# Weight sums of seven-product matrices made by accumulating transfers, with the signs moved to the other operand

## The reference, cut to what matters

```python
def sqrelu_mlp(h, w_up, w_down):
    a = jax.nn.relu(h @ w_up)
    return (a * a) @ w_down

def reference(x, ...):
    for i in range(DEPTH):                       # DEPTH = 2
        h = rmsnorm(x, norm_mix[i])
        x = x + (short_conv_mixer(...) if i % 2 == 0 else neighborhood_attention_2d(...))
        h = rmsnorm(x, norm_mlp[i])
        x = x + sqrelu_mlp(h, mlp_w_up[i], mlp_w_down[i])
    return rmsnorm(x, norm_final)
```

## Time and profile before

| | us |
|---|---|
| median of three runs | 1042.34 |
| the three runs | 1042.2, 1042.34, 1044.16 |
| span of the profiled execution, first to last instruction | 1041.8 |
| PE busy in it | 1032.3 |
| DVE busy | 846.8 |
| ACT busy | 598.4 |
| POOL busy | 103.6 |

### The profile page before, as it was taken

How to read it: one execution, slowest core, us unless ns; L and a number is a source line. 1 busy time by engine, 2 the same in 40 slices (tenths; PEclk the granted TensorE clock), 3 DMA queues, 4 the chain that set the end, 5 groups by cost and what they waited for, 6 DMA issues and landing times.

```text
span 1041.8 us, 15414 instructions
## 1 busy us (share of the span) xinstructions
PE 1032.3 (99%) x6104; PEld 905.4 (87%) x6104; DVE 846.8 (81%) x1185; ACT 598.4 (57%) x836; POOL 103.6 (10%) x158
## 2 busy tenths in 40 slices
PE   9999999999999999999999999999999999999997
PEld 8888888988998998998878888889888988988985
DVE  5876688699899689688987767797799798698697
ACT  6222347665584574575765655547664674674675
POOL 3453001000000000000113000000000000000003
PEclk9999999999999999999999999999999999999999
DMA  7998568326745645633998733157056547447423
GB/s 247 375 375 300 141 165 254 108 42 207 204 132 176 177 128 177 181 97 102 372 249 249 215 90 114 55 191 274 1 122 205 163 133 202 150 134 202 147 51 111
DMA packets 36998, 182.71 MB, mean 175 GB/s; under 512 B 5760, under 2 KB 5888, under 8 KB 22848
## 3 DMA queue, kind: packets, MB, share of 16 engines
q1 hardware_dynamic: 23184, 108.57, 28.8%
q0 software_dynamic: 13456, 72.64, 28.3%
q10 hardware_dynamic: 288, 0.52, 0.2%
HBM read 136.93 MB, written 27.32 MB: 158 GB/s over the span
## 4 chain that ended last, share of the span: by engine, by line
PE 93%; DVE 4%; DMA 1%; ACT 1%; issue 1%; POOL 0%; DVEq 0%; POOLq 0%; ACTq 0%
PE bank L770 29%; PE bank L771 29%; PE bank L772 29%; DMA raw<-sevens 1%; PE bank L975 1%; PE bank L953 1%; DVE w_l L1514 1%; PE bank L938 1%; PE bank L793 1%; DVE xs L1661 1%; PE bank L997 0%; DVE big L1970 0%; ACT big L1156 0%; DVE a_l L1727 0%; ACT w_h L1128 0%
## 5 line engine op out<-in xcount | busy, mean ns | idle before, releaser
L1128 ACT ACTIVATE w_h<-big 128x1024 fp32r<-128x1024 f32 x210 | 221.7, 1058 | 216.0 <-PE bank L772 215.0
L770 PE MATMUL bank<-a_h,w_h 128*128 128x256 f32 (+1 forms) x892 | 295.0, 331 | 0.0
L772 PE MATMUL bank<-a_h,w_l 128*128 128x256 f32 (+1 forms) x892 | 292.9, 328 | 0.0
L771 PE MATMUL bank<-a_l,w_h 128*128 128x256 f32 (+1 forms) x892 | 292.8, 328 | 0.0
L1514 DVE TENSOR_TENSOR w_l<-big,w_h 128x1024 fp32r<-128x1024 f32 x210 | 252.0, 1225 | 21.8 <-ACT w_h L1128 21.8
L770 PE MATMUL bank<-w_h,hx 128*128 128x512 f32 x568 | 222.1, 391 | 0.8 <-ACT big L1376 0.4
L771 PE MATMUL bank<-w_l,hx 128*128 128x512 f32 x568 | 221.2, 389 | 0.0
L772 PE MATMUL bank<-w_h,hx 128*128 128x512 f32 x568 | 221.0, 389 | 0.0
L770 PEld LDWEIGHTS bank<-a_h,w_h 128*128 128x128 f32 x892 | 169.6, 190 | 15.8 <-issue 0.2
L772 PEld LDWEIGHTS bank<-a_h,w_l 128*128 128x128 f32 x892 | 169.6, 190 | 15.0
L771 PEld LDWEIGHTS bank<-a_l,w_h 128*128 128x128 f32 x892 | 169.6, 190 | 14.7 <-issue 0.2
(11 more groups left out here) (193 smaller groups left out, 1253.6 us busy)
## 6 DMA issues: line engine op xcount, KB each, us to landing
big<-blocks SPq DMA_DIRECT2D x56, 1024.0 KB, 5.0
big<-big POOLq DMA_DIRECT2D x30, 1024.0 KB, 7.0
raw<-weights SPq DMA_DIRECT2D x52, 512.0 KB, 6.6
raw<-t_sums SPq DMA_DIRECT2D x16, 512.0 KB, 3.7
t_sums<-sevens POOLq DMA_DIRECT2D x6, 1024.0 KB, 12.6
t_sums<-t_sums POOLq DMA_DIRECT2D x6, 1024.0 KB, 12.2
raw<-sevens SPq DMA_DIRECT2D x12, 512.0 KB, 7.8
bias_tiles<-big POOLq DMA_DIRECT2D x8, 632.0 KB, 9.3
```

The lines of the kernel that those rows point to most:

```text
L770: nc.tensor.matmul(dst, sh, mh, start=start, stop=False, skip_group_check=again)
L771: nc.tensor.matmul(dst, sh, ml, start=False, stop=False, skip_group_check=again)
L772: return nc.tensor.matmul(dst, sl, mh, start=False, stop=stop, skip_group_check=again)
L1128: nc.scalar.activation(wh_all[:, w % SLOTS, :], src, ACT.Copy).then_inc(w_hi, 1)
```

## The change

The signs of the scheme are moved so that every sum of weights is a plain addition, and the subtractions fall on the operand sums and on the additions into the output (`ALU.subtract` in `evict` and `add`, `scale=-1.0` in one ReLU). The weight sums are now T1 = Y12 + Y11, T2 = T1 + Y22, T3 = Y12 + Y22 and T4 = Y21 + T2.

- T1 is made by POOL as an accumulating transfer of Y11 into Y12 (`first_sum`), for q+1 behind `add_sums(q)` in POOL's order.
- T2 stays with DVE (`sum_of_y`) in the same place; it now waits for the landing of T1's transfer.
- T3: once P1 has consumed Y11, POOL loads Y12 a second time from DRAM into the room of Y11, waits for it, and accumulates Y22 onto it.
- T4 is as before, but behind the longer T3 in POOL's order.

```diff
-                                  "P3": ("Y22", *loaded(q, "Y22")), "P5": ("Y12", t_sum, 2 * q + 1),
-                                  "P6": ("T2", t_sum, 2 * q + 2), "P7": ("Y11", t3_in, 16 * (q + 1)),
+                                  "P3": ("Y22", *loaded(q, "Y22")), "P5": ("Y12", t1_in, 16 * (q + 1)),
+                                  "P6": ("T2", t_sum, q + 1), "P7": ("Y11", t3_in, 16 * (q + 1)),
...
+            def first_sum(q):
+                at = ROOMS[q]
+                pool.wait_ge(*loaded(q, "Y12"))
+                pool.wait_ge(*loaded(q, "Y11"))
+                pool.dma_start(room[at["Y12"]], room[at["Y11"]], accum_op=ALU.add).then_inc(t1_in, 16)
+
             def add_sums(q):
                 at = ROOMS[q]
-                pool.wait_ge(t_sum, 2 * q + 2)
+                pool.wait_ge(t1_in, 16 * (q + 1))
                 pool.wait_ge(w_split, part_end(q, "P1"))
-                pool.dma_start(room[at["Y11"]], room[at["T2"]], accum_op=ALU.add).then_inc(t3_in, 16)
+                pool.dma_start(room[at["Y11"]], blocks[q, Y_ROLES.index("Y12")]).then_inc(y_again, 16)
+                pool.wait_ge(*loaded(q, "Y22"))
+                pool.wait_ge(y_again, 16 * (q + 1))
+                pool.dma_start(room[at["Y11"]], room[at["Y22"]], accum_op=ALU.add).then_inc(t3_in, 16)
+                pool.wait_ge(t_sum, q + 1)
                 pool.wait_ge(w_split, part_end(q, "P2"))
                 pool.dma_start(room[at["Y21"]], room[at["T2"]], accum_op=ALU.add).then_inc(t4_in, 16)
...
+            first_sum(0)
             negative_in(0, 0)
...
             for q in range(1, SEQ_ATTN):
+                first_sum(q)
                 add_sums(q)
...
-            def sums_of_y(q, i):
+            def sum_of_y(q):
                 at = ROOMS[q]
-                if i == 0:
-                    dve.wait_ge(*loaded(q, "Y12"))
-                    dve.wait_ge(*loaded(q, "Y11"))
-                    nc.vector.tensor_tensor(room[at["Y12"]], room[at["Y12"]], room[at["Y11"]], ALU.subtract).then_inc(t_sum, 1)
-                else:
-                    ...
-                    nc.vector.tensor_tensor(room[at["T2"]], room[at["Y12"]], room[at["Y22"]], ALU.subtract).then_inc(t_sum, 1)
+                dve.wait_ge(*loaded(q, "Y22"))
+                if q:
+                    dve.wait_ge(w_split, part_end(q - 1, "P4" if q in (1, SEQ_ATTN) else "P3"))
+                    dve.wait_ge(t3_in, 16 * q)
+                dve.wait_ge(t1_in, 16 * (q + 1))
+                nc.vector.tensor_tensor(room[at["T2"]], room[at["Y12"]], room[at["Y22"]], ALU.add).then_inc(t_sum, 1)
+
+            def minus_both(dst, left, right):
+                return nc.vector.scalar_tensor_tensor(out=dst, in0=left, scalar=-1.0, in1=right, op0=ALU.mult, op1=ALU.subtract)
...
-                nc.vector.tensor_tensor(S2[:, k, :], hraw[:, k, left], S1[:, k, :], ALU.subtract).then_inc(chain, 1)
+                minus_both(S2[:, k, :], hraw[:, k, left], S1[:, k, :]).then_inc(chain, 1)
...
-                    nc.vector.tensor_tensor(x11, x11, x22, ALU.subtract).then_inc(sb_ready, 1)
+                    minus_both(x11, x11, x22).then_inc(sb_ready, 1)
...
-                    if pos == 3:
-                        sums_of_y(q + 1, 0)
```

More of the change, by code:

```diff
@@ L422, in encoder @@
         y_in = {role: sem(f"{role}_in") for role in Y_ROLES}
+        t1_in = sem("t1_in")
+        y_again = sem("Y12_again")
         t3_in = sem("t3_in")
@@ L1206, in relu_square @@
             def relu_square(tb, i, src, dst):
-                nc.scalar.activation(dst, src, ACT.Relu).then_inc(c_relu, 1)
+                nc.scalar.activation(dst, src, ACT.Relu, scale=-1.0 if i in (1, 2) else 1.0).then_inc(c_relu, 1)
                 act.wait_ge(c_relu, 4 * tb + i + 1)
@@ L1536, in sums_of_x @@
                 steps[0] = steps[0] + 1
-                nc.vector.tensor_tensor(S1[:, k, :], hraw[:, k, right], hraw[:, m, right], ALU.add).then_inc(chain, 1)
+                nc.vector.tensor_tensor(S1[:, k, :], hraw[:, m, right], hraw[:, k, right], ALU.subtract).then_inc(chain, 1)
                 x_first(tc, m)
@@ L1540, in sums_of_x @@
                 steps[0] = steps[0] + 1
-                nc.vector.tensor_tensor(S2[:, k, :], hraw[:, k, left], S1[:, k, :], ALU.subtract).then_inc(chain, 1)
-                nc.vector.tensor_tensor(hraw[:, k, right], hraw[:, k, right], hraw[:, k, left], ALU.subtract)
+                minus_both(S2[:, k, :], hraw[:, k, left], S1[:, k, :]).then_inc(chain, 1)
+                nc.vector.tensor_tensor(hraw[:, k, right], hraw[:, k, left], hraw[:, k, right], ALU.subtract)
                 dve.wait_ge(chain, steps[0])
-                nc.vector.tensor_tensor(hraw[:, m, left], hraw[:, m, left], S2[:, k, :], ALU.add).then_inc(s_ready, 1)
+                minus_both(hraw[:, m, left], hraw[:, m, left], S2[:, k, :]).then_inc(s_ready, 1)
             def x_rest(tc, pos):
@@ L1577, in in_sums @@
                 elif i == 1:
-                    nc.vector.tensor_tensor(t1, t0, t1, ALU.add).then_inc(in_sum, 1)
-                    link(nc.vector.tensor_tensor(t0, t0, u_part("P1", False).bitcast(f32), ALU.subtract))
+                    nc.vector.tensor_tensor(t1, t1, t0, ALU.subtract).then_inc(in_sum, 1)
+                    link(nc.vector.tensor_tensor(t0, u_part("P1", False).bitcast(f32), t0, ALU.subtract))
                 elif i == 2:
-                    nc.vector.tensor_tensor(t0, t0, u_part("P1", True).bitcast(f32), ALU.subtract).then_inc(in_sum, 1)
+                    nc.vector.tensor_tensor(t0, t0, u_part("P1", True).bitcast(f32), ALU.add).then_inc(in_sum, 1)
                 elif i == 3:
@@ L1585, in in_sums @@
                 elif i == 4:
-                    nc.vector.tensor_tensor(t1, t0, t1, ALU.subtract).then_inc(in_sum, 1)
+                    minus_both(t1, t0, t1).then_inc(in_sum, 1)
                 elif i == 5:
@@ L1590, in in_sums @@
                 else:
-                    nc.vector.tensor_tensor(t0, t0, t1, ALU.add).then_inc(in_sum, 1)
+                    minus_both(t0, t0, t1).then_inc(in_sum, 1)
             def in_rest(n, i):
@@ L1616, in s_block @@
                     dve.wait_ge(xb_ready, 4 * tb + 3)
-                    nc.vector.tensor_tensor(x22, x21, x22, ALU.add).then_inc(sb_ready, 1)
+                    nc.vector.tensor_tensor(x22, x22, x21, ALU.subtract).then_inc(sb_ready, 1)
                 elif i == 1:
-                    nc.vector.tensor_tensor(x21, x21, x11, ALU.subtract).then_inc(sb_ready, 1)
+                    nc.vector.tensor_tensor(x21, x11, x21, ALU.subtract).then_inc(sb_ready, 1)
                 elif i == 2:
                     dve.wait_ge(sb_ready, 4 * tb + 1)
-                    nc.vector.tensor_tensor(x11, x11, x22, ALU.subtract).then_inc(sb_ready, 1)
+                    minus_both(x11, x11, x22).then_inc(sb_ready, 1)
                 else:
                     dve.wait_ge(sb_ready, 4 * tb + 3)
-                    nc.vector.tensor_tensor(x12, x12, x11, ALU.add).then_inc(sb_ready, 1)
+                    minus_both(x12, x12, x11).then_inc(sb_ready, 1)
             def up_seven(n, c):
@@ L1638, in up_seven @@
                     if pos == 5:
-                        sums_of_y(q + 1, 1)
+                        sum_of_y(q + 1)
                     if pos == 6:
@@ L1654, in up_seven, with add @@
                         x_block(tc, "P1")
-            def add(index, t, f, b):
+            def add(index, t, f, b, negative=False):
                 if index > 1:
@@ L1660, in add @@
                 cols = slice(512 * f, 512 * f + 512)
-                nc.vector.tensor_tensor(xs[:, t, cols], bank[b][:], xs[:, t, cols], ALU.add).then_inc(adds, 1)
+                if negative:
+                    nc.vector.tensor_tensor(xs[:, t, cols], xs[:, t, cols], bank[b][:], ALU.subtract).then_inc(adds, 1)
+                else:
+                    nc.vector.tensor_tensor(xs[:, t, cols], bank[b][:], xs[:, t, cols], ALU.add).then_inc(adds, 1)
             def evict(tc, pos):
@@ L1675, in evict @@
                     src = banks[:, 512 * b:512 * b + 1024].rearrange("p (t n) -> p t n", t=2)
-                    nc.vector.tensor_tensor(dst, src, dst, ALU.add).then_inc(adds, 2)
+                    nc.vector.tensor_tensor(dst, dst, src, ALU.subtract if f else ALU.add).then_inc(adds, 2)
                     return
@@ L1679, in evict @@
                 for t in range(2):
-                    add(adds_after(tc, name) - (4 if both else 2) + t, 2 * half + t, f, b + t)
+                    add(adds_after(tc, name) - (4 if both else 2) + t, 2 * half + t, f, b + t, f == 1)
                 if both:
@@ L1748, in second @@
                     if pos == 5:
-                        sums_of_y(seq_of(tc) + 1, 1)
+                        sum_of_y(seq_of(tc) + 1)
                     evict(tc, pos)
-                    if pos == (4 if tc in BY_UNIT else 3) and n is None:
-                        sums_of_y(seq_of(tc) + 1, 0)
                     lo(first + 2 * pos + 4)
```

(8 more changed lines are left out.)

## The result

The changed kernel takes 1078.05 us (median of four runs, 1076.77 to 1081.31) against 1042.37: the ratio is 1.0338 (95% interval 1.0324 to 1.0352), slower by 35.7 us. The forecast was 1046.5 in a range up to 1056. The profiled execution took 1079.02 us and has a span of 1077.2.

The account below looks back on a forecast made before the run. PE was taken as the bound, busy 1032.3 of 1041.8 us, so relieving DVE counted 0. To the median 1042.3 came 4.1 us of stalls from late T1 transfers, rounded to 1046.5 us; range 1041.6 to 1056.

Parts of the forecast that it names:

- the 2 us that the prediction took as cover: P7 of INNER matrices: ACT's lead over PE, taken as 2 us of real cover for a late T3, costed at nothing.
- rival C: P7 of INNER matrices: T3 lands late, 1 to 2 us in four matrices besides the 4.1, about 1050; chance 0.13.
- The rival without a stall (B): T2 at matrix starts: chain 29.9 to 31 us, each lateness under its cover, 1042.3 within 1041.3 to 1044; chance 0.35.
- the sum of the upper bounds (D, 1056): Matrix starts: loads cost T1 4.5 us, late places pay 7.6 more, four in-time places 2.0, giving 1056; chance 0.08.
- The place-by-place sum: Starts of q2, q3, q9, q10: stalls 0.5, 1.2, 1.1 and 0.9, plus 0.4 for later P1 splits, 4.1 us.
- The four places that it had in time by 0.9 us: q4 to q5 and the ends of q6, q11, q13: T1 at 373.7, needed at 374.56, so no stall.
- I take 2.6 us: T1's transfer beside SP's loads of Y22 and Y21: loses 2.6 us, some six tenths of a 4.5 us overlap.
- the row's 4.5 us: Earlier trace, accumulate at 233.07 with one load beside it: 11.5 in place of 7.0 us, taken as T1's upper bound.
- all four late places: T2 after q1, q2, q8, q9: T1 late by 0.7, 1.6, 1.35, 1.3 us; stalls 0.5, 1.2, 1.1, 0.9.
- T1 of an up projection ... three products of time lie between it and T2: q5 to q6: T1 issued right behind T4 meets the loads too, but three products cover it; costed at nothing.
- 5.1 + 0.3 + 7.0 + 5.2 + ...: From T3's old issue through T3, T4 and Y11's load to T1's landing: 29.9 us, with 2.6 for loads 32.5.
- A stall was priced at its own length: PE at the late places: lateness less cover counted as the loss, with PE's work keeping the same pace.

## Why the prediction was wrong

**Right.** What bounds the kernel, and that 34.2 us off DVE are worth nothing; the chain from T3's old issue over T4 and the load of Y11 to T1, and T2 as the place where it is paid, which the runs with T1 or T3 alone, with T4 first and with T2 later bear out; that the signs are free; that T3 itself is covered. Here the outcome was right and the size wrong. T3's accumulate landed 10.0 us after its issue in q3 and q5, 11.4 in q10 and 12.0 in q12, ACT waited 2.6, 2.6, 3.7 and 4.8 us for it, more than the 2 us that the prediction took as cover, and PE lost nothing at P7. So the condition of rival C came true and its price did not. ACT in order of time, the split of P7 of q12:

```profile
966.71 2.01 ACT L1144 ACTIVATE w_h<-big 128x1024 fp32r<-128x1024 f32 x2 [4.80 <-DMA big<-big]
```

The rival without a stall (B) fell too, and so did the sum of the upper bounds (D, 1056): the range lacked 22 us.

**The place-by-place sum**, 4.1 us for 35.4, failed in four steps. The four places that it had in time by 0.9 us cost 16.3 of the 35.4; the first three steps made them late.

*"I take 2.6 us"*, the share that T1 loses to SP's loads. The transfer of T1 for q5 took 10.9 us in place of 9.6, the one for q2 12.9. DMA issue in a narrow window, changed kernel, T1 of q2:

```profile
big<-big POOLq DMA_DIRECT2D x1, 1024.0 KB, 12.9
```

It also went out at 250.5, not 249.8, and landed 4 us later than forecast. T1 of q5 lost 3.9 us against the 7.0 of the earlier trace rows. T1 of q2 lost 5.9: beside it ran the end of Y22 (landed at 252.5), Y21 (landed at 256.7) and then the first load for q3. That passed the row's 4.5 us. The upper bound that I had drawn from one row with one load was not an upper bound for several.

The prediction weighed a price of 2.4 us for a whole load, by the fit and the alternation that the Trainium skill states ("DMA: Bandwidth & Descriptors", sections on the anatomy of one DMA and on SWDGE, HWDGE and iDMA); this case's trace shows 4.5 us. Its sum by that price was wrong too: with six tenths of 2.4 us, 1.4, in place of 2.6, all four late places fall within their cover, and the sum is 1042.3, not 1045.7.

*"T1 of an up projection ... three products of time lie between it and T2"*, cost nothing. It cost PE nothing by itself, but it made the next chain late. DMA issues in narrow windows around 330.8 (T4 of q3 and T1 of q4 together, median) and at 331.5 (T1 of q4 alone):

```profile
big<-big POOLq DMA_DIRECT2D x2, 1024.0 KB, 11.6
big<-big POOLq DMA_DIRECT2D x1, 1024.0 KB, 15.2
```

DVE in order of time, T2 of q4, the splits of P1 of q4, and T2 of q5:

```profile
346.68 2.29 DVE L1576 TENSOR_TENSOR big<-big 128x2048 f32<-128x2048 f32 x1 [2.51 <-DMA big<-blocks]
350.02 2.36 DVE L1530 TENSOR_TENSOR w_l<-big,w_h 128x1024 fp32r<-128x1024 f32 x2
387.89 2.29 DVE L1576 TENSOR_TENSOR big<-big 128x2048 f32<-128x2048 f32 x1 [3.94 <-DMA big<-big]
```

At q4 T4, T1, Y22 and Y21 move at once. T1 took 15.2 us and the load of Y22 12.4. PE did not notice, but T2 of q4 waited 2.5 us for Y22, and behind it the split of P1 ended at 352.38: 11.7 us later than before, where PE was 9.3 later. So the chain to q5 started 2.4 us late. T2 of q6, q11 and q13 waited for a load by SP too (2.5, 1.4 and 1.9 us), ahead of the chains to q7, q12 and q14; the sum for these was not redone. The forecast had all four in time by 0.9 us. I had asked whether PE feels each transfer, not whether the next chain does.

*"5.1 + 0.3 + 7.0 + 5.2 + ..."*, the links. In q4: the load landed 5.1 us after its issue, POOL took 0.5 us to issue (forecast 0.3), T3 7.7 (7.0), T4 4.9 behind it (5.2), Y11 4.9, POOL 0.5, T1 10.9: 34.8 us for 32.5. Of the five transfers in line two were slower, T3 by 0.7 and T1 by 1.3 us, and POOL's two issues took 0.2 us more each. With the 2.4 us of the late start it gives 4.7 us: T2 of q5, in time by 0.9 us in the forecast, waited 3.9, and PE lost 3.4 of them. POOL in order of time, changed kernel:

```profile
352.97 0.56 POOL L658 DMA_DIRECT2D big<-blocks  x1 [20.92 <-DVE w_l L1530]
358.63 0.86 POOL L661 DMA_DIRECT2D big<-big  x1 [5.10 <-DMA big<-blocks]
359.19 1.18 POOL L664 DMA_DIRECT2D big<-big  x1
376.82 0.85 POOL L651 DMA_DIRECT2D big<-big  x1 [16.45 <-DMA big<-blocks]
```

*A stall was priced at its own length.* At q2 PE stood still for 4.3 us and lost 6.8, as the granted clock was 0.50 behind it; with q10 and q14 the clock cost some 6 us of the 35.4. That PE's work keeps its pace was a condition that the prediction named, and it did not hold. PE's busy time alone doesn't show it: in the run with T2 later it grew by 5.4 us at a granted clock of 1.00 up to 1041.9 us, by many short waits.

What was not forecast at all, 1.5 us at unit 188: T1 of q8 shares with the load of plain weights (L595), which landed 15.4 us after its issue. DMA issues in the window 724.6:724.8, changed kernel:

```profile
big<-big POOLq DMA_DIRECT2D x1, 1024.0 KB, 14.7
raw<-weights SPq DMA_DIRECT2D x1, 512.0 KB, 15.4
```

It is there with T1 by transfer (1.3, 1.8, 1.8 and 1.6 us in four more runs, but under 0.5 us in the run with T4 ahead of T3 in all NORMAL matrices) and gone in every run with T1 of q8 by DVE. The 1.3 us elsewhere in the attention comes and goes from run to run and isn't explained.

## What to carry to other kernels

When a fast engine's work is handed to a chain of transfers, ask not only whether each is covered but what each does to the start of the next chain: here places that were each in time by a microsecond all became late. A price for sharing must be taken with as many transfers in flight as there will be; one load beside one accumulate is no bound for two. And where the matrix engine is 99% busy, relief of another engine buys nothing, while a queue with some 0.6 us of cover turns every late wait into lost time: look first at what stands behind the wait, as moving one instruction gave back two thirds.

## What the runs showed of the hardware

- An accumulate of 1 MB took 7.0 us alone, 7.9 beside the end of one load, 10.9 with loads beside it all the time (T1 of q5), 12.9 likewise (T1 of q2), and 15.2 behind another accumulate and beside two loads; the load of Y22 beside the last took 12.4 us in place of 4.9.
- After a stop of PE of 4.3 us (start of q2) its granted clock was 0.50 in the next stretch, and it fell to that level after one of 2.9 us at q10 too; after one of 3.4 us at q12 it stayed at 1.00, and after 1.9 us at q9 as well (2.1 lost). So the length of the last stop alone does not decide it. PE in order of time, the first products of q10 and q12:

```profile
863.80 0.77 PE L786 MATMUL bank<-w_h,hx 128*128 128x512 f32 x1 [2.88 <-DVE hx L1624]
947.41 0.47 PE L786 MATMUL bank<-w_h,hx 128*128 128x512 f32 x1 [3.35 <-DVE hx L1624]
```

- POOL issues an accumulate 0.5 us after the landing of the load that it waits for.
- The combined multiply and subtraction takes 1219 ns at 1024 elements, no more than the plain kind (1217). The dearer rows at 512 elements have a scale per partition as their scalar, this one a constant. The kernel before has the kind with a constant at 512 elements as well, at 682 ns against the 684 of the plain kind, which the prediction overlooked; the two differ in their tiles too, so the scalar as the reason isn't isolated. Group by line and shape, kernel before:

```profile
L1954 DVE SCALAR_TENSOR_TENSOR sx<-bank,sx 128x512 fp32r<-128x512 f32 x8 | 5.5, 682 | 0.0
```
